# Two halves of the tokens: U for the last 256 first, then U and a native fp32 V of the first 256 beside fetched V rows for the last 256

## The reference

```
h2 = modulate(rms_norm(x, g2), sh2, sc2)                  # 512 x 1024
# 8 heads; per head the 16 best of 128 x 128 experts, from two top-16 lists
g = softmax(top_s)                                        # 512 x 8 x 16 weights
u = eu[it]                                                # rows of a 16384 x 1024 table
a = gelu(einsum('ckd,cd->ck', u, ht)) * gt
out = einsum('ck,kd->cd', a, ev[it])                      # rows of a second such table
x = x + g2[:, None, :] * out
```

## Time and profile before

| | us |
|---|---|
| median of three runs | 1734.19 |
| the three runs | 1730.11, 1734.19, 1737.25 |
| the profiled execution, its own time | 1722.75 |
| its span | 1720.7 |
| granted TensorE clock, mean share of full | 0.982 |

### The profile page before, as it was taken

The page is one execution under the profiler, slowest core; times in us unless marked ns, Lnnn a source line. Parts: engine busy times, 40 slices in busy tenths (PEclk is TensorE's granted clock), DMA queues, the critical chain, the costliest instruction groups (busy, mean ns, idle before and its releaser), DMA issues.

```text
span 1720.7 us, 24837 instructions
## 1 busy us (share of the span) xinstructions
PE 1678.6 (98%) x8253; PEld 1460.2 (85%) x8253; DVE 1167.8 (68%) x1962; ACT 623.2 (36%) x906; POOL 765.0 (44%) x460
## 2 busy tenths in 40 slices
PE   6999999999999999999999999999999998999999
PEld 3776667788888888888888888889999998999999
DVE  7585547678999242675675765305887777798888
ACT  3544432333444432333333333333333333333332
POOL 4432114233544444333333333447888887422221
PEclk9899999899999999999999999999999999999999
DMA  7324336122444443556555566557998898999995
GB/s 294 126 74 148 114 130 235 60 86 82 145 146 146 146 143 133 178 195 205 183 178 184 177 197 212 204 194 283 339 325 311 313 310 317 392 388 342 348 347 186
DMA packets 167858, 366.32 MB, mean 213 GB/s; under 512 B 16896, under 2 KB 82560, under 8 KB 167680
## 3 DMA queue, kind: packets, MB, share of 16 engines
q1 hardware_dynamic: 145280, 298.54, 50.3%
q0 software_dynamic: 22528, 67.19, 10.9%
HBM read 304.85 MB, written 60.82 MB: 213 GB/s over the span
## 4 chain that ended last, share of the span: by engine, by line
PE 77%; POOL 12%; DVE 4%; issue 3%; DMA 3%; ACT 0%; DVEq 0%; SPq 0%; ACTq 0%; PEldq 0%; POOLq 0%
PE ps L1309 17%; PE ps L1310 17%; PE ps L1311 17%; POOL coef L577 9%; PE ps L1590 5%; PE ps L1589 5%; PE ps L1591 5%; POOL rows L573 4%; PE ps L1549 3%; DVE adasum L895 1%; DMA rows<-w_stream,row_at 1%; PE ps L1438 1%; PE ps L1456 1%; PE ps L1520 1%; PE ps L1378 1%
## 5 line engine op out<-in xcount | busy, mean ns | idle before, releaser
L544 POOL TENSOR_TENSOR wlo<-raw,whi 128x1024 fp32r<-128x1024 f32 x180 | 445.3, 2475 | 703.5 <-ACT whi L612 703.5
L1309 PE MATMUL ps<-ahi,whi 128*128 128x512 f32 x1296 | 509.2, 393 | 0.2 <-DVE zbuf L989 0.2
L1310 PE MATMUL ps<-alo,whi 128*128 128x512 f32 x1296 | 506.9, 391 | 0.0
L1311 PE MATMUL ps<-ahi,wlo 128*128 128x512 f32 x1296 | 506.3, 391 | 0.0
L612 ACT ACTIVATE whi<-raw 128x1024 fp32r<-128x1024 f32 x304 | 322.0, 1060 | 367.5 <-PE ps L1591 323.8
L1589 PE MATMUL ps<-phi,whi 128*128 128x384 f32 x1024 | 346.8, 339 | 10.7 <-DVE plo L1244 10.7
L1590 PE MATMUL ps<-plo,whi 128*128 128x384 f32 x1024 | 345.2, 337 | 0.0
L1591 PE MATMUL ps<-phi,wlo 128*128 128x384 f32 x1024 | 345.0, 337 | 0.0
L1311 PEld LDWEIGHTS ps<-ahi,wlo 128*128 128x128 f32 x1296 | 244.5, 189 | 51.5
L1309 PEld LDWEIGHTS ps<-ahi,whi 128*128 128x128 f32 x1296 | 244.8, 189 | 49.8 <-issue 0.7
L1310 PEld LDWEIGHTS ps<-alo,whi 128*128 128x128 f32 x1296 | 244.7, 189 | 48.5
(11 more groups left out here) (216 smaller groups left out, 1519.5 us busy)
## 6 DMA issues: line engine op xcount, KB each, us to landing
raw<-w_stream SPq DMA_DIRECT2D x304, 512.0 KB, 3.9
gelu_spill<-gout SPq DMA_DIRECT2D x128, 256.0 KB, 2.3
ada<-w_ada SPq DMA_DIRECT2D x48, 512.0 KB, 5.8
gate_spill<-gblock SPq DMA_DIRECT2D x12, 2048.0 KB, 7.8
gates<-gate_spill SPq DMA_DIRECT2D x32, 768.0 KB, 6.8
gin<-gelu_spill SPq DMA_DIRECT2D x128, 192.0 KB, 7.2
xt<-x_t SPq DMA_DIRECT2D x1, 2048.0 KB, 7.8
rows<-w_stream,row_at POOLq DMA_INDIRECT x128, 6.1
```

Of the source, the lines that this page charges most:

```text
L544: g.tensor_tensor(wlo[:, s, :], raw[:, s, :], whi[:, s, :].bitcast(F32), ALU.subtract)\
L1309: mm(out, shi, mhi, start=n == 0, stop=False)
L1310: mm(out, shi, mlo, start=False, stop=False)
L1311: last = mm(out, slo, mhi, start=False, stop=n == len(pairs) - 1)
```

## The change

The tokens are cut into two halves of 256.

First stretch: U for the last 256 tokens only, in 128 chunks; the gelu goes to `gelu_spill`, now half as wide. The picks of tokens 0 to 255 are made first, and their weights are scattered (32 groups between the chunks 36 and 99). The picks of tokens 256 to 511 follow after the scatter.

Second stretch: per chunk, U is loaded, split and multiplied again, for the first 256 tokens (`again`); its gelu stays in SBUF, is multiplied with the gates (`make_prod`) and used at once by a V chunk in native float32: 8 matmuls of 256 columns, V loaded into a ring of its own (`values_in`) without a split. Beside it the V rows of the last 256 tokens are fetched: 256 indirect DMAs of rows and 256 of gelu values, with 12 rows in flight. At the end eight output tiles are read in two halves each.

```
-DENSE = 3 * P
-ROWS = 8
+HALF = T // 2
+PAIR = TT // 2
+ROWS = 12
+COEFS = 4
-U_A2, U_B, U_C = 36, 44, 116
-BODY_CHUNKS = 12
+U_A2, U_T, U_B, U_C = 30, 32, 36, 100
+BODY_CHUNKS = 16
 # SP
+            def load_again(e, s):
...
+                    sp.wait_ge(u_lo_ready, e - (POOL_LO + RING - 1))
+                sp.dma_start(raw[:, s % RING, :], w_front[C_U + e]).then_inc(raw_loaded[s % RING], 16)
+            def values_load(e, s):
+                if not isinstance(e, int) or e >= RING:
+                    sp.wait_ge(values_used, e - (RING - 1))
+                sp.dma_start(values_in[:, s % RING, :], w_front[C_E + e]).then_inc(values_loaded[s % RING], 16)
+            def v_step(e, s, chunk=True, values=True, group=None):
+                if values:
+                    values_load(e + 3, s + 3)
+                if chunk:
+                    load_again(e + 7, s + 7)
                 if group is not None:
+                    sp.wait_ge(prod_ready, e + 1)
                     gate_load(group, s // GROUP % 2)
 # GpSimd
             for e in range(POOL_LO):
                 lo_part(C_E + e, e)
+            pool.wait_ge(places_ready, 1)
+            for m in range(ROWS):
+                fetch_row(m)
             for s in range(RING):
                 pool.wait_ge(gelu_stored[s], 16 * (NK // RING + 1))
+            ahead = 4 * COEFS
+            for m in range(ahead):
+                fetch_coef(m)
+            for m in range(ROWS, PAIR * NK):
+                fetch_row(m)
+                k = m - ROWS + ahead
+                if k < PAIR * NK:
+                    fetch_coef(k)
 # ScalarE
+            def v_step(e, q, s, chunk=True):
+                act.wait_ge(chunk_used, e + (C_E + 1))
+                if not isinstance(e, int) or e >= RING:
+                    act.wait_ge(prod_ready, e - (RING - 1))
...
+                a.activation(gout[:, s, :], ps[:, 6 + s % 2, 0:HALF], ACT.Gelu).then_inc(gelu_done, 1)
+                if chunk:
+                    again_split(e + RING, q + 1, s)
 # VectorE
+            pick_experts(0)
+            pick_experts(1, last=True)
+            weights_normed(0).then_inc(gates_ready, 1)
...
+            dve.wait_ge(scat_done, 4 + 2 * GROUPS)
+            pick_experts(2)
+            pick_experts(3, last=True)
...
+            def make_prod(e):
+                g, s = e // GROUP, e % GROUP
+                dve.wait_ge(gelu_done, NK + 3 + e)
+                if s == 0:
+                    dve.wait_ge(gate_in[g % 2], 16 * (g // 2 + 1))
+                if e >= RING:
+                    dve.wait_ge(values_used, e - RING + 1)
+                v.tensor_tensor(prod[:, e % RING, :]..., gout[:, e % RING, :]..., gates[...], ALU.mult)
+            def rows_done(e):
+                return max(0, e - BEHIND) * NK // (NK - BEHIND)
             for e in range(NK):
+                make_prod(e)
+                if e + RING < NK:
+                    again_lo(e + RING)
...
+                for n in range(rows_done(e), rows_done(e + 1)):
+                    dve.drain()
+                    add_rows(n)            # one row for each of the two 128-token tiles
 # TensorE
+            def v_tile(e, q, s, first=False, final=False):
+                pe.wait_ge(prod_ready, e + 1)
                 slot = s % RING
+                pe.wait_ge(values_loaded[slot], 16 * (q + 1))
                 for j in range(DK):
+                    last = mm(ps[:, j // 2, j % 2 * HALF:(j % 2 + 1) * HALF], values_in[:, slot, column(j)],
+                              prod[:, slot, :], start=first and j % 2 == 0, stop=final, skip_group_check=True)
+                    if final and j % 2 == 1:
+                        if j == 1:
+                            pe.wait_ge(row_added, PAIR * NK)
+                            pe.wait_ge(gelu_done, 2 + 2 * NK)
...
+            def again(e, s):
+                u_tile(e + NK, s, tokens=slice(0, HALF), again=True)
             with pe.Fori(1, NK // RING - 1) as i:
                 for s in range(RING):
+                    again(i * RING + (s + 1), s + 1)
+                    v_tile(i * RING + s, i, s)
```

More of the change, by code:

```diff
@@ L207, in build @@
[L207 to L217, removed]
@@ L316, in build @@
         row_in = [sem(f"row_in{s}") for s in range(ROWS)]
[L317 to L318 removed]
+        coef_in = [sem(f"coef_in{b}") for b in range(COEF_RING)]
+        u_lo_ready = sem("u_lo_ready")
         row_added = sem("row_added")
@@ new lines, in scale_coefs, with add_rows @@
+            def scale_coefs(b):
+                dve.wait_ge(coef_in[b % COEF_RING], 16 * PAIR * COEFS * (b // COEF_RING + 1))
+                some = slice(b * COEFS, (b + 1) * COEFS)
+                v.tensor_tensor(coef[:, :, some], coef[:, :, some], gate_of[:, :, some], ALU.mult)
+                dve.drain()
+            def add_rows(n):
+                if n % COEFS == 0:
+                    scale_coefs(n // COEFS)
+                for t in range(PAIR):
+                    m = n * PAIR + t
+                    dve.wait_ge(row_in[m % ROWS], 16 * (m // ROWS + 1))
+                    row, factor = rows[:, m % ROWS, :], coef[:, t, n:n + 1]
+                    if n == 0:
+                        v.tensor_scalar(acc[:, t, :], row, factor, None, ALU.mult).then_inc(row_added, 1)
+                    else:
+                        v.scalar_tensor_tensor(acc[:, t, :], row, factor, acc[:, t, :], ALU.mult, ALU.add)\
+                         .then_inc(row_added, 1)
@@ L1533, in _, with u_tile @@
             pe.wait_ge(mod_ready, 6)
-            def u_tile(e, s):
+            def u_tile(e, s, tokens=slice(HALF, T), again=False):
                 pe.wait_ge(gelu_done, e + 1)
-                pe.wait_ge(lo_ready, e + (C_U + 1))
-                product(ps[:, 6 + s % 2, :], [(weights(s % RING, k), (ahi[:, k, :], alo[:, k, :])) for k in range(DK)])\
+                if again and (not isinstance(e, int) or e >= NK + POOL_LO):
+                    pe.wait_ge(u_lo_ready, e - (NK + POOL_LO - 1))
+                else:
+                    pe.wait_ge(lo_ready, e + (C_U + 1))
+                product(ps[:, 6 + s % 2, 0:HALF],
+                        [(weights(s % RING, k), (ahi[:, k, tokens], alo[:, k, tokens])) for k in range(DK)])\
                     .then_inc(chunk_used, 1)
```

366 lines of the change are left out of this document (154 added, 212 removed).

## The result

The changed kernel took 1765.15 us (median of 4 runs, 1759.15 to 1777.85) beside 1734.43 for the kernel before (4 runs, 1730.11 to 1737.25): ratio 1.019, 95% interval 1.0153 to 1.0226. It is 1.9% slower, where 1687 us was forecast. The profiled execution took 1763.6 us, its span 1761.7.

The account below looks back on a forecast made before the run. TensorE, busy 98% of the span, was taken as the bound. From 417.63, a first stretch of 399, a second of 848 and a tail of 9 gave span 1674; adding 2.05 gave 1676, adding 11.4 gave 1687 us; range 1660 to 1724.

Parts of the forecast that it names:

- Before, 17 us of 549 were lost to such couplings; now 12 instead, bounds 0 and 40.: Second stretch: loss to waits between VectorE's product, the gelu, row additions and GpSimd's rows, taken as 12 us.
- 16 x 0.225: Second stretch: a V chunk's 16 native fp32 records at 0.225 us, midway between 0.2167 and 0.2333, make 3.60 us.
- 0.08 per chunk: Second stretch: extra time of the first product after a native group, 0.08 us per chunk, +10 us in all.
- The first stretch: U for 128 chunks plus the scatter of 256 tokens: 399 us with 3 of stall, ending at 817.
- 34.9 each: First stretch: time of each VectorE pick in us; picks 3 and 4 would end by 807 to 815, hidden behind TensorE.
- GpSimd's low part fits: First stretch: GpSimd's low part takes 2.61 us against 2.85 for a TensorE chunk, 0.2 to spare.
- U at 256 columns: Both stretches: products at 0.1188 us each, 2.85 per chunk, both halves 730 us against 696 before, +33.
- Rival C: 256-column products slower than 0.119 in long rows, or first stretch held by GpSimd and SP; 1737 us at 0.127; chance 0.08.
- Rival A: Second stretch: GpSimd's 512 indirect DMA issues become the bound, from 1.59 us per issue on; 1707 us; chance 0.18.
- Rival B: Second stretch: DMA engines become the bound if about 317 GB/s is all they carry; 1751 us, slower; chance 0.14.
- The tail: Kernel end: 9 us beyond the last chunk, for late row additions, 16 closing operations and the last store.
- TensorE's granted clock falls there again and again: Second stretch: a sign that, if seen, would show the forecast wrong; no size given.

Follow-up runs that it names:

- changed_again: The changed kernel, unaltered, as a control on a chip without stalls: 1655.0 us (two runs) beside 1720.0 for the kernel before, ratio 0.962.
- changed_third: The changed kernel, unaltered, run again on a chip with stalls: 1727.4 and 1760.3 us, beside 1725.1 for the kernel before.
- smooth: Changed kernel with gathers issued after TensorE's U and V chunks, two or three rows added per chunk, additions two chunks later: 1661.5 us, ratio 0.964 to before.
- half_low: smooth with GpSimd's low part of the first stretch's U chunks 512 instead of 1024 columns wide (U not exact): 1648.6 us beside 1730.6, ratio 0.953.
- no_rows: The changed kernel without 244 of its 256 row gathers, the same twelve rows added again and again: 1652.8 us.
- changed_fourth: The changed kernel, unaltered, as control on a chip without stalls: 1652.2 us beside 1720.9 for the kernel before.
- paced: Changed kernel with GpSimd's gathers issued only in step with TensorE's chunks and row additions two chunks later: 1654.1 us beside 1720.9 for the kernel before.

## Why the prediction was wrong

The deviations, in us of the profiled executions, for the chip of the result and for one without stalls:

```
                                     forecast    after   changed_again
start of U                              417.6    419.4       414.8
U start to first V product              405.2    421.0       420.7
first V product to start of chunk 126   834.8    905.6       799.5
start of chunk 126 to the span's end     16.2     15.7        15.7
span                                     1674   1761.7      1650.8
```

- **The step that failed** is "Before, 17 us of 549 were lost to such couplings; now 12 instead, bounds 0 and 40." On the chips that stall it is 108 us in after (905.6 less 126 x 6.33 = 797.6) and 109 in changed_third. I had looked for loss in waits between named instructions only; this one has none. The runs show in its place gaps in which TensorE waits for no one (63 us) and the half clock behind them, in rows of GpSimd's gathers, and smooth, in which TensorE's progress stops GpSimd, loses 8.1 on a chip with stalls. In changed_again it is 1.9 us, and there the change is faster than I said: 1655.0 lies below my range of 1660 to 1724.
- **A chunk of the second stretch** was forecast at 6.53 and is 6.33. The term "16 x 0.225" was too dear: native records of 256 columns are 0.216 apart, just below my lower end of 0.2167. The "midway" was not needed, for the kernel before has two records of this width, which I had read only in the sum of eight of different widths:

```profile
151.39 0.59 PE L1456 MATMUL ps<-probs_t,vt 128*64 128x256 f32 x2
...
151.82 0.38 PE L1456 MATMUL ps<-probs_t,vt 128*64 128x128 f32 x2
```

- The "0.08 per chunk" for the change of kind is nothing (2.88 for U, 24 x 0.12). I had read it off 417.63 to 417.94 and counted twice: the last native record there starts at 417.60, so 0.34 us are its own 0.11 and the next product's 0.227. Together with 2.88 instead of 2.85 for U that is 25 us less in 126 chunks.
- **The first stretch** was forecast at 399 and lost 15.8 us. TensorE waits for 11.7, where I had allowed 3; some 4 are the chunks at 2.88 instead of 2.85; the rest, about 3, goes with the half clock in 518 to 525 us, behind the first of these waits. The term that failed is "34.9 each" for the picks, taken from a kernel in which GpSimd was half idle: beside one that is busy for 90% they take 44 to 44.7, the first two end too late for the transposes (4.4, inside my 0 to 8), and the last two, which I had called hidden, end after TensorE's chunks. That GpSimd's low part fits was right as far as TensorE waits 1.1 us for it, though it took 2.86 and not 2.61. half_low shows one cause behind all this. The Trainium skill, GPSIMD Engine Reference, Key points, with the two engines in contention for shared SBUF interfaces, agrees with it; I used that rule for the second stretch alone, where it did not matter.
- **U at 256 columns** was right: 23 products in 2.75 us (1056.61 to 1059.36 in changed_again), 0.120 each against 0.1188. Rival C's dear products are out; its "first stretch held by GpSimd" was real only by way of the picks. The row decided rightly over the rule of N/2.4 + 2.5 ns (the Trainium skill, TensorE: Matmul & The Clock Gate, Back-to-back issue gap), by which it would be 0.109. That section gives the rule for an isolated product and says that the weight loads of a stream set its spacing as well, which I had left out.
- **Rival A** (issues bound): no. GpSimd's issues in the long rows of changed_again are 1.34 to 1.41 apart in the mean, not the 1.48 that I extrapolated, and it waits 64 us for VectorE; without the coefficient gathers nothing is won.
- **Rival B** (DMA bound) gave 1751, near the 1765, for a wrong reason: the 311 GB/s of after are what is left when TensorE stalls. The same kernel carries 358 and, with more asked, 387; with half the load (no_rows, 186 GB/s in 1050 to 1350) it takes 1652.8, no less than changed_fourth's 1652.2 on another chip without stalls. The 387 passed for 100 us. The 358 GB/s of the Trainium skill, Perfetto Trace Analysis, Engine Utilization, which I took for the peak, are by the same section a core's share when both cores of a pair draw; one core alone may pass it, up to about 435 GB/s, and the trace agrees.
- **The tail** came out at 15.7 against 16.2.
- Of my signs, "TensorE's granted clock falls there again and again" was the one that came (0.76 in 850 to 900). It follows a stall and is not its start: it falls after TensorE's gaps (the first at 856.9, the clock at 859.8).

What stays open: what it is on a chip that lets GpSimd's gathers slow TensorE's and SyncE's instructions. The DMA packets take the same time on both kinds of chip (a row piece of 4 KB 0.16 us in the median), and every chip ran the same program. Open too is what else the changed kernel must have for it, for the kernel before, with its 200 gathers in a row, lost 7.6 us to it where the changed one lost 109. Whether the coefficients' 4-byte packets matter more than the rows was not met on a chip with stalls.

## What to carry to other kernels

Run the unaltered kernel as a control on the same chip before you read a cure; here the change is 4% faster on two chips, 1 to 2% slower on two others, and on a fifth its two runs were 1727.4 and 1760.3 beside 1727.9. Take the time of a product from single starts inside its group: a merged row counts the change to its neighbour with it. smooth, 0.964 of before on a chip where the unaltered change is 1.010, is the version to keep; on a chip without stalls only its coarser sibling was run (paced, 1654.1 beside the changed kernel's 1652.2). An engine that issues gathers should be stopped by the engine that bounds the kernel, not only by its own ring: then, if my reading is right, a stall cannot feed itself. A duration read beside a half-idle neighbour is a lower end once that neighbour is full.

## What the runs showed of the hardware

- While GpSimd issues indirect DMAs in a row (0.30 us idle between two), on some chips TensorE's products and SyncE's instructions come 0.7 us apart or multiples of it, in the first such stall of after with the DMA engines nearly idle at its end (0.07 in 870 to 883 us); it ends when GpSimd pauses. Other chips take 52 such gathers in a row without it.
- Native fp32 products of 128x128 weights by 256 columns: two records each, 0.216 us apart, 3 ns above 2 x 256 / 2.4 GHz. fp32r products of 256 columns: 0.120 apart. Going from one kind to the other and back costs nothing measurable in a chunk of 6.33 us.
- A VectorE operation of 0.22 us takes 2.28 beside GpSimd's subtraction of 1024 columns and ends with it, and 1.24 beside one of 512 columns (half_low). The subtraction itself goes from 2.41 us (600 to 740 us, VectorE on the scatter) to 2.86 (747 to 840 us, the picks).
